# Where the weight buffers start in the partition: one offset constant from 16 to 48 words

## What is computed

```python
# block 1
h    = rmsnorm(x) * (1 + scale1) + shift1          # scale, shift, gate: silu(c) @ w_ada
proj = h @ w_in                                    # q, k, v, gates, indexer, latents
y    = (sigmoid(za) * (gla @ w_branch_a) + sigmoid(zb) * (dsa @ w_branch_b)) @ w_out
x    = x + gate1 * y
h2   = rmsnorm(x) * (1 + scale2) + shift2
# PEER: 8 heads x 16 experts of 16384 per token, gathered by row
u, v = expert_u[ix], expert_v[ix]
a    = gelu(einsum('td,thkd->thk', h2, u)) * gates
x    = x + gate2 * einsum('thk,thkd->td', a, v)
# block 2
z    = rmsnorm(x) @ w_in_2                         # 4608 columns
x    = x + (g_a * (conv_a @ w_a_out) + g_b * (conv_b @ w_b_out)) @ w_o
u    = rmsnorm(x) @ w_up                           # 5632 columns
x    = x + (gelu(conv(u[:, :2816])) * u[:, 2816:]) @ w_down
x    = x + sigmoid(rmsnorm(x) @ w_ple_gate) * (p @ w_ple)
out  = rmsnorm(x)
```

## Time and profile before

| what | value |
|---|---|
| median of 3 runs | 1355.08 us |
| span of the profiled execution (its own time is not listed apart) | 1351.9 us |
| TensorE matmul busy | 1213.3 us (90%) |
| weight loads busy | 908.6 us (67%) |
| VectorE busy | 1059.9 us (78%) |
| ScalarE / GpSimd busy | 616.6 / 285.6 us |
| read from HBM | 414.52 MB |

### The profile page before, as it was taken

How to read it: one execution, slowest core, us unless ns; L and a number is a source line. 1 busy time by engine, 2 the same in 40 slices (tenths; PEclk the granted TensorE clock), 3 DMA queues, 4 the chain that set the end, 5 groups by cost and what they waited for, 6 DMA issues and landing times.

```text
span 1351.9 us, 19486 instructions
## 1 busy us (share of the span) xinstructions
PE 1213.3 (90%) x6950; PEld 908.6 (67%) x6950; DVE 1059.9 (78%) x2159; ACT 616.6 (46%) x1265; POOL 285.6 (21%) x278
## 2 busy tenths in 40 slices
PE   8999999999989877778877777778899999999998
PEld 5999999999743332324322322323599999999998
DVE  6898678878879777777766777777699978899666
ACT  4666555656334333332433333233563264554445
POOL 1010000002545544344344434443000000000000
PEclk9999999999999999999999999999999999999999
DMA  9966546665999999999999999999843534554461
GB/s 389 383 226 249 187 158 236 237 217 233 382 424 427 427 428 427 427 428 427 427 427 427 427 427 427 428 428 427 357 174 139 187 130 183 187 187 173 174 237 41
DMA packets 55200, 416.64 MB, mean 308 GB/s; under 512 B 6081, under 2 KB 6721, under 8 KB 8658
## 3 DMA queue, kind: packets, MB, share of 16 engines
q0 software_dynamic: 36864, 268.45, 47.2%
q1 hardware_dynamic: 17792, 146.51, 29.3%
q10 hardware_dynamic: 466, 0.63, 0.1%
HBM read 414.52 MB, written 1.05 MB: 307 GB/s over the span
## 4 chain that ended last, share of the span: by engine, by line
DMA 28%; PE 28%; DVE 6%; issue 3%; ACT 3%; POOL 1%; DVEq 0%; ACTq 0%; POOLq 0%
DMA ring<-in_experts,rowid 28%; PE ps L1092 5%; PE ps L755 5%; PE ps L756 5%; PE ps L757 5%; PE ps L1244 1%; PE ps L1245 1%; PE ps L1243 1%; DVE ring L2360 1%; DVE h_rows L2360 1%; PE ps L748 1%; DVE w_lo L1942 1%; ACT w_hi L1329 1%; PE ps L1200 1%; ACT arena L1592 0%
## 5 line engine op out<-in xcount | busy, mean ns | idle before, releaser
L1092 PE MATMUL ps<-arena 128*128 128x512 f32 x512 | 234.4, 603 | 56.9 <-ACT arena L1596 56.7
L1092 PE MATMUL ps<-ring,arena 128*128 128x512 f32 x440 | 211.2, 628 | 48.8 <-ACT arena L1596 48.7
L2360 DVE CUSTOM_DVE_ANT_0 arena<-arena 128x1024 f32<-128x1024 f32 x128 | 151.6, 1223 | 99.1 <-DMA arena<-in_experts,rowid 96.4
L1092 PEld LDWEIGHTS ps<-arena 128*128 128x128 f32 x512 | 92.8, 189 | 193.5 <-ACT arena L1596 97.3
L658 POOL DMA_INDIRECT arena<-in_experts,rowid x128 | 128.7, 1005 | 353.4 <-DVE rowid L2287 192.8
L1092 PEld LDWEIGHTS ps<-ring,arena 128*128 128x128 f32 x440 | 85.2, 200 | 170.1 <-issue 90.8
L757 PE MATMUL ps<-h_hi,w_lo 128*128 128x256 f32 x700 | 194.6, 278 | 0.0
L1589 ACT ACTIVATE arena<-arena 128x2 f32<-128x2 f32 x126 | 25.6, 203 | 366.4 <-DVE arena L2360 361.3
L755 PE MATMUL ps<-h_hi,w_hi 128*128 128x256 f32 x672 | 188.4, 280 | 2.7 <-DVE w_lo L1942 2.1
L756 PE MATMUL ps<-h_lo,w_hi 128*128 128x256 f32 x672 | 186.7, 278 | 0.0
L2360 DVE CUSTOM_DVE_ANT_0 ring<-ring,arena 128x1024 f32<-128x1024 f32 x112 | 133.4, 1223 | 36.8 <-DMA ring<-in_experts,rowid 27.4
(11 more groups left out here) (419 smaller groups left out, 2559.0 us busy)
## 6 DMA issues: line engine op xcount, KB each, us to landing
ring<-in_early_w SPq DMA_DIRECT2D x43, 1024.0 KB, 4.9
arena<-in_ada_w SPq DMA_DIRECT2D x24, 1024.0 KB, 8.5
arena<-in_up_w SPq DMA_DIRECT2D x11, 2048.0 KB, 7.8
arena<-in_z_w SPq DMA_DIRECT2D x8, 2048.0 KB, 7.7
arena<-in_down_w SPq DMA_DIRECT2D x8, 1408.0 KB, 5.9
arena<-in_o_w SPq DMA_DIRECT2D x2, 2048.0 KB, 7.9
arena<-in_early_w SPq DMA_DIRECT2D x3, 1024.0 KB, 6.5
arena<-in_experts,rowid POOLq DMA_INDIRECT x128
```

The lines of the kernel that those rows point to most:

```text
L1092: mm = pe.matmul(BK[4 + 2 * t + b], diag[:, j, :], rows[j][:, D + b * 512:D + (b + 1) * 512], start=first and j == 0, stop=last and j == ( ...
L2360: v.tensor_tensor_reduce(out=u, in0=u, in1=h2tok[:, t, :], scale=1.0, scalar=0.0, op0=ALU.mult, op1=ALU.add, accum_out=dots[:, even, j:j + ...
```

## The change

`ASIDE` becomes 48 words. Every buffer that starts `ASIDE` past a multiple of 64 words starts 32 words (128 bytes) later in the partition: the weight chunks, their high and low parts, the expert rows, `diag`, `pacc`, `s_all`, `sT`, `scb`, `zg`, `scc`. `LINE - ASIDE` shrinks by the same 32 words, so that the split activations stay where they are. The total size stays.

```diff
@@ -254,7 +254,7 @@
         stat = sb("stat", [P, 2, T])
 
         SIZE = 28352
-        LINE, ASIDE = 64, 16
+        LINE, ASIDE = 64, 48
 
         def overlay(*tensors):
 
```

## The result

The changed kernel takes **1372.53 us** (median of 4 runs, 1372.13 to 1373.03), the kernel before 1354.61 us beside it (4 runs, 1353.32 to 1355.50): a ratio of 1.0133 [1.0119, 1.0148]. It is slower by 18 us, outside the forecast range of 1347 to 1363 us. The profiled executions differ by 19.4 us in span (1351.9 and 1371.3 us).

A forecast was written before the change was run, and what follows sets the result against it. TensorE was taken to bound the first 300 us or so and after 970 us, expert-row DMAs at 427 GB/s between. All terms summed to 0: span 1351.9 us plus 3.2 us gave 1355.0 us, range 1347 to 1363 us.

The forecast's parts named there:

- the row DMAs taken at 0: Expert-row and weight loads landing 128 bytes past a multiple of 256: no cost, judged from `ada_w` loads at 423 GB/s.
- the 256-column products taken at 0: TensorE products, moving operand going from 64 bytes below to 64 above the weights: same two paces as before, 0 us.
- Rival D: Row stage: DMA writes starting in the middle of 256 bytes take one more piece in 32, +19 us, 1374 us; chance 0.03.
- its sign, under 420 GB/s: Row-stage DMA rate in the new profile that would show the extra-piece cost of writes starting in the middle of 256 bytes.
- The bounds: 256-column products: all at 113.3 ns would give -7.5 us, all at 117.6 ns +11.2 us.
- ±64 are mirror images: 256-column products: if the memory pattern repeats every 128 bytes, 64 below and 64 above are equivalent; nothing changes, 0 us.
- The first step of a start: TensorE stretches: the two starts shown differ by the first step, 220 against 190 ns, and each stretch keeps its pace.
- Rival B: Long `up` and `down` stretch of 1450 matmuls locks in slow: +6.4 us, 1358 to 1366 us; chance 0.22.
- The Trainium skill's rule of two read ports: TensorE: loading the next weights takes no read bandwidth from the running matmul, so addresses cannot matter; sum 0.
- VectorE insensitive: VectorE dots: the distance of two operands costs nothing, 1223 against 1222 ns; taken as 0.
- L1092 no cost: TensorE at L1092: `diag` and `rows` move together, distance stays 0, stage bound by DMA; 0.
- the 384 matmuls of the queries: Query products, slices moving from 64..8 bytes below to 64..120 above: 1.9 us won or lost, taken as 0.

The follow-up runs named there:

- the first base experiment: Changed kernel with the 128-byte tensor `topu` moved behind the big buffers, everything else 128 bytes lower, distance kept: 1363.32 us, 1.0075 of the kernel before.

## Why the prediction was wrong

**Two steps failed: the row DMAs taken at 0, and the 256-column products taken at 0.**

*DMA into weights and rows, taken at 0.* The rows paid, and the `ada_w` loads were the wrong witness for them. With rows at 0 (the first base experiment) the row stage runs at 427 GB/s, in all versions that start them at 64, 128 or 192 at 422. An 8 KB packet of the rows takes 309.1 ns in the mean in the one case and 313.8 or 313.9 in all three others, which is 8.4 of the 9.7 us by which the middle third grew. The `ada_w` loads and `xT` land 192 bytes past a multiple of 256 in the kernel before, and yet 417 of the 484 packets of 8 KB in its first 12 us take 309 ns (five such loads, 640 packets, were issued ahead of the first weight chunk). The view of 8 to 12 us shows the same:

```profile
DMA packets 227, 1.70 MB, mean 424 GB/s; under 512 B 17, under 2 KB 20, under 8 KB 20
q1 hardware_dynamic: 227, 1.70, 100.5%
```

100.5% of 16 engines over 4 us are 64.3 us, by 207 large packets some 311 ns. So the step read these loads rightly, no price at 192, and carried it over to the rows wrongly. No run shows what the start of a stream costs. Nor could 423 against 427 have told: a window of 6 us holds some 310 large packets, and three packets more or less are the 4 GB/s. The 418 against 423 GB/s from 6 to 12 us above are some 4 packets as well; from 8 to 12 us the changed kernel has 427 against 424. The price is not one of the rows' queue alone: between 12 and 70 us, where the early weight chunks now land at 128, the share of SyncE's 8 KB packets that take 309 ns fell from 84% to 58%, while between 70 and 330 us it stayed at 84 to 85%. What decides which packets pay stays open. Rival D named the place of the writes, at 19 us and a chance of 0.03; its size was off by a factor of two, and its sign, under 420 GB/s, did not show.

The Trainium skill's rule ("DMA: Bandwidth & Descriptors", "How a descriptor splits into AXI transactions"), which speaks of what is read, has a descriptor off a 256-byte boundary take its first transaction from the boundary below. For 8 KB that is 33 transactions for 32, and by its beats of 32 bytes an estimate of 260 for 256 (1.6%) at 128, 258 (0.8%) at 64 and 262 (2.3%) at 192. The runs bear out that the boundary of 256 bytes matters on the writing side too, in the row DMAs, at 1.5% a packet; that the price is the same at 64, 128 and 192 does not fit the estimate.

*The 256-column products, taken at 0 between -7.5 and +11.2.* The bounds were right: the two paces were the only ones at this distance, and the outer thirds lost 2.5 + 7.2 = 9.7 us, near the upper bound. The choice between the bounds was wrong. It rested on "±64 are mirror images", which the whole table above contradicts, and on `product_tok` at 113.4 ns. That stretch showed that a rhythm once entered is kept at 64 above, as I noted, and not that it is entered there. The first step of a start doesn't tell the pace either, as the prediction had it from two starts: the changed kernel's long stretch takes 224 ns for its first step, the fast one before 223, and goes on at 117.8. The changed kernel shows the other half: one stretch of some 380 matmuls starts at 117.3 ns and turns to 113.5 when the distance turns to 64 below.

*Rival B* (slower by the start of the long stretch, 0.22) named the largest single piece, 6.4 us. It was priced alone; in the end nearly all stretches went with it.

*The Trainium skill's rule of two read ports* ("TensorE: Matmul & The Clock Gate", Part 2, step 1) gave 0 for the products. The trace's objection to it stands: with weights and rows at one address and only the activations moved, the same matmul takes 113.3 to 120.0 ns. How the two streams meet, the runs don't say.

*What held:* VectorE insensitive (1223 ns for the expert dot before and after); L1092 no cost (most starts 429 ns apart before and after); the 384 matmuls of the queries, without a visible change (a median of 282 ns in both views above, and 21.3 us from the first to the last start); and the reading that TensorE's pace goes nearly in full into the end outside the row stage: the 1451, 191, 190 and 106 matmuls of the second block that turned slow, less 142 that turned fast, are 7.9 us, and the second block grew by 7.2.

*The sum as it should have been:* 9.7 us (middle third, 8.4 of them by the rate of the rows, the rest open) + 9.7 us (products at 117.7 ns) = 19.4 us on the span; by the medians 18 us.

## What to carry to other kernels

Where a change moves only addresses, look for the stages that are full, and take a witness of the same kind for each: the first loads of another queue showed no price for a place that cost the rows 1.5% a packet, and over a stage of 640 us one per cent is 6 us. Read a difference of one per cent from packet times or from hundreds of microseconds, not from a window of 6. Where such transfers fill the queues, try their destinations on a multiple of 256 bytes, and measure the distance between moving and stationary operand as its own parameter: among eight distances the same kernel went from about 1354 to 1383 us, some 9 of them for the place of the rows. Where a kernel's runs scatter by several microseconds, look for a stretch that can settle in two rhythms before trusting a single profile of it.

## What the runs showed of the hardware that I had not expected

- The indirect row DMAs, 8 KB a partition, written from a multiple of 256 bytes: 427 GB/s, 309.1 ns a packet; from 64, 128 or 192 past it: 422 GB/s, 313.8 or 313.9 ns. The first loads of SyncE's queue, 192 past it, take 309 ns in 417 of 484 packets.
- Matmuls of 256 columns with a weight load each, back to back at the full clock, settle at 113.3 or 117.7 ns with the moving operand 64 bytes below the stationary one, mostly at 117.7 with it 64 above, at 120.0 at distance 0 or 96 above. Which operand is the weight and which the activation makes no difference: the sign of the distance does.
- The rhythm is there within some five matmuls of a start (steps of 224, 118, 117, 118 ns in the changed kernel's long stretch) and lasted 1450 matmuls; a small extra matmul at the start changed it for 550 that followed, in three profiles of three. That one program takes either in different executions is inferred from its two groups of times, 6.9 us apart.
